# Expert weights loaded in halves: 1 MB transfers with a wait and a release for each half

## The reference, cut to what matters

```
for i in range(DEPTH):                      # 2 layers
    h = rmsnorm(x, norm_mix_g[i])
    x = x + (retention_mixer(h, ...) if i == 0 else conformer_conv_mixer(h, ...))
    h = rmsnorm(x, norm_ffn_g[i])
    x = x + hierarchical_moe(h, ...)        # 32 experts, each token goes to 2 of them
# for each expert e and each of its blocks of tokens:
    (silu(xblk @ w_gate[e]) * (xblk @ w_up[e])) @ w_down[e]   # 1024 -> 512 -> 1024
```

## Time and profile before

| | us |
|---|---|
| median of 3 runs (lowest, highest) | 1625.94 (1623.56, 1627.71) |
| the profiled execution's own time | 1625.24 |
| its span, first to last instruction | 1623.4 |
| TensorE busy | 1495.5 (92%) |
| VectorE busy | 989.1 (61%) |
| mean of the 16 DMA engines on the main queue | 67.4% of the span |

### The profile page before, as it was taken

One profiled execution on the slowest core, in us unless ns is written; L12 is line 12 of the kernel. 1 busy time (PEld: TensorE's weight loads), 2 busy tenths in 40 slices (PEclk: granted clock), 3 DMA queues, 4 the chain that ended last, 5 costly groups with the idle time before them and its releaser, 6 DMA issues.

```text
span 1623.4 us, 45311 instructions
## 1 busy us (share of the span) xinstructions
PE 1495.5 (92%) x18938; PEld 982.5 (61%) x18939; DVE 989.1 (61%) x1662; ACT 446.2 (27%) x731; POOL 423.7 (26%) x371
## 2 busy tenths in 40 slices
PE   7999999999989999998789899979999988889996
PEld 5868778688645555554445588747555555445553
DVE  4222022220378888776566889952788877668877
ACT  5242422322432222221112422154222212112222
POOL 3434334244101212121111255523021211112121
PEclk9999999999999999999999999999999999999998
DMA  9212212122299999999999620116399999999996
GB/s 377 85 64 71 93 53 104 52 104 104 87 377 428 429 428 428 429 428 428 429 429 426 277 100 20 41 57 266 118 417 430 428 429 429 428 428 430 428 428 271
DMA packets 33849, 457.60 MB, mean 282 GB/s; under 512 B 3840, under 2 KB 3968, under 8 KB 6400
## 3 DMA queue, kind: packets, MB, share of 16 engines
q1 hardware_dynamic: 33648, 456.57, 67.4%
q10 hardware_dynamic: 144, 0.18, 0.0%
HBM read 454.64 MB, written 2.10 MB: 281 GB/s over the span
## 4 chain that ended last, share of the span: by engine, by line
PE 66%; DMA 21%; DVE 10%; issue 1%; ACT 1%; SPq 0%; POOL 0%; DVEq 0%; ACTq 0%
PE ps L803 15%; PE ps L697 9%; PE ps L699 9%; PE ps L698 9%; DMA area_b<-w_gu 9%; PE ps L820 8%; PE ps L739 7%; PE ps L786 5%; DMA ring<-w_down 5%; DMA ring<-w_gu 4%; DVE area_c L1321 4%; DMA hT<-w_down 3%; PE ps L888 2%; DVE ring L1321 2%; PE ps L880 1%
## 5 line engine op out<-in xcount | busy, mean ns | idle before, releaser
L1159 DVE TENSOR_TENSOR x<-x,ps 128x1024 f32<-128x1024 f32 x384 | 450.9, 1216 | 90.7 <-PE ps L786 90.7
L456 POOL TENSOR_SCALAR slot_tok<-trig,slot_now 128x512 fp32r<-128x512 f32 x94 | 147.0, 1563 | 710.7 <-PE ps L786 710.7
L425 POOL TENSOR_TENSOR w_lo<-ring,w_hi 128x512 fp32r<-128x512 f32 x176 | 236.8, 1348 | 359.4 <-ACT w_hi L475 359.2
L803 PE MATMUL ps<-ring,hgT 128*32 128x256 f32 x4160 | 259.5, 391 | 48.4 <-DMA ring<-w_gu 28.6
L803 PEld LDWEIGHTS ps<-ring,hgT 128*32 128x32 f32 x4160 | 131.1, 111 | 145.0 <-issue 41.1
L475 ACT CAST w_hi<-ring 128x512 fp32r<-128x512 f32 x176 | 108.9, 623 | 346.8 <-PE ps L699 346.3
L739 PE MATMUL ps<-area_a,block_rows 128*32 128x256 f32 x3072 | 187.7, 386 | 0.6 <-DVE block_rows L1120 0.6
L549 ACT ACTIVATE y_hi<-ps,slots 128x256 fp32r<-128x256 f32 x94 | 44.5, 474 | 396.7 <-PE ps L820 396.7
L739 PEld LDWEIGHTS ps<-area_a,block_rows 128*32 128x32 f32 x3072 | 102.3, 113 | 72.1 <-issue 9.5
L820 PE MATMUL ps<-ring,aT_e 128*32 128x256 f32 x2080 | 125.7, 382 | 3.6 <-DMA ring<-w_down 3.6
L697 PE MATMUL ps<-w_hi,hT_hi 128*128 128x512 f32 x320 | 125.0, 391 | 2.9 <-DVE hT_lo L1351 2.9
(11 more groups left out here) (216 smaller groups left out, 1941.5 us busy)
## 6 DMA issues: line engine op xcount, KB each, us to landing
ring<-w_gu SPq DMA_DIRECT2D x88, 2048.0 KB, 28.1
ring<-w_down SPq DMA_DIRECT2D x44, 2048.0 KB, 29.0
area_c<-w_gu SPq DMA_DIRECT2D x20, 2048.0 KB, 29.3
area_b<-w_gu SPq DMA_DIRECT2D x20, 2048.0 KB, 31.8
hT<-w_down SPq DMA_DIRECT2D x20, 2048.0 KB, 32.4
ring<-w_pw SPq DMA_DIRECT2D x6, 2048.0 KB, 10.8
ring<-w_qk SPq DMA_DIRECT2D x4, 2048.0 KB, 8.4
ring<-w_v SPq DMA_DIRECT2D x4, 2048.0 KB, 8.7
```

What stands on the lines that cost most here:

```text
L425: nc.gpsimd.tensor_tensor(w_lo[:, place, :], ring[:, s, at:at + 512], w_hi[:, place, :].bitcast(F32), ALU.subtract).then_inc(lo_ready, 1)
L456: nc.gpsimd.tensor_scalar(slot_tok[:, :], tok_number, slot_now[:, 0:1], None, ALU.is_equal).then_inc(tok_hot[l], 1)
L803: last = nc.tensor.matmul(ps[32 * g:32 * g + 32, 2, 0:256], hgT[:, n * (KT // 2) + k, :], gate_up[n][:, k, :, g * P:(g + 1) * P], start=(n ...
L1159: return V.tensor_tensor(x[:, i, :].rearrange("p (g c) -> p g c", g=4), x[:, i, :].rearrange("p (g c) -> p g c", g=4), ps[:, bank:bank + 4 ...
```

## The change

Each expert load is cut in two of 1 MB: the first 2048 of the 4096 columns of a place ("front") and the last 2048 ("back"). The front ends on a new semaphore `front_loaded` of the place, the back on `slot_loaded`. TensorE waits for the front before the first half of its 16 matmuls on a place, and for the back before the second half. It counts up a new semaphore after each first half (`gu_first`, `gu_third`, `y_half`), and SyncE waits for that before the front of the later expert and for the old one before its back. The loads of retention and convolution weights are as before.

```
@@ sync queue @@
+            def load_front(s, w):
+                sp.dma_start(places[s][:, 0:SLOT // 2], w[:, 0:SLOT // 2]).then_inc(front_loaded[s], 16)
+            def load_back(s, w):
+                sp.dma_start(places[s][:, SLOT // 2:SLOT], w[:, SLOT // 2:SLOT]).then_inc(slot_loaded[s], 16)
+            def load_halves(s, w):
+                load_front(s, w)
+                load_back(s, w)
...
-                    load_slot(s, w[l, e])
+                    load_halves(s, w[l, e])
...
+                        sp.wait_ge(gu_first[l], upto)
+                        load_front(s_gu0, gu0_l[bass.ds(e * P, P), :])
                         sp.wait_ge(gu_half[l], upto)
-                        load_slot(s_gu0, gu0_l[bass.ds(e * P, P), :])
+                        load_back(s_gu0, gu0_l[bass.ds(e * P, P), :])
+                        sp.wait_ge(gu_third[l], upto)
+                        load_front(s_gu1, gu1_l[bass.ds(e * P, P), :])
                         sp.wait_ge(gu_mm[l], upto)
-                        load_slot(s_gu1, gu1_l[bass.ds(e * P, P), :])
+                        load_back(s_gu1, gu1_l[bass.ds(e * P, P), :])
+                        sp.wait_ge(y_half[l], upto)
+                        load_front(s_down, down_l[bass.ds(e * P, P), :])
                         sp.wait_ge(y_mm[l], upto)
-                        load_slot(s_down, down_l[bass.ds(e * P, P), :])
+                        load_back(s_down, down_l[bass.ds(e * P, P), :])
@@ tensor engine, one_block @@
-                    pe.wait_ge(slot_loaded[s], 16 * turn + (expert_base(l, s) + 16))
+                    pe.wait_ge(front_loaded[s], 16 * turn + (front_base(l, s) + 16))
                     for k in range(KT // 2):
+                        if k == KT // 4:
+                            last.then_inc((gu_first, gu_third)[n][l], 1)
+                            pe.wait_ge(slot_loaded[s], 16 * turn + (expert_base(l, s) + 16))
...
-                pe.wait_ge(slot_loaded[s_down], 16 * turn + (expert_base(l, s_down) + 16))
+                pe.wait_ge(front_loaded[s_down], 16 * turn + (front_base(l, s_down) + 16))
                 for k in range(4):
+                    if k == 2:
+                        last.then_inc(y_half[l], 1)
+                        pe.wait_ge(slot_loaded[s_down], 16 * turn + (expert_base(l, s_down) + 16))
```

More of the change, by code:

```diff
@@ L219, in program @@
         slot_loaded = sems("slot_loaded", 3 * DEPTH)
+        front_loaded = sems("front_loaded", 3 * DEPTH)
         x_loaded = sems("x_loaded", NT)
@@ L266, in program @@
             both(n) for n in ("slots_hot", "slots_spread", "tok_loaded", "slot_known", "tok_hot", "y_split", "y_rounded", "first_mm", "second_mm", "added"))
-        gu_half = both("gu_half")
+        gu_first, gu_half, gu_third, y_half = (both(n) for n in ("gu_first", "gu_half", "gu_third", "y_half"))
         hgT_ready, gu_mm, silu_ready, act_ready, aT_ready, y_mm = (
@@ L277, in expert_base, with front_base @@
             return after_ret[s] + l * (16 * experts + in_conv[s])
+        def front_base(l, s):
+            return l * 16 * len(range(s // 3, NE, DEPTH))
         slots_of = [(0, 1, 2), (3, 4, 5), (6, 7, 8)]
@@ L351, in _ @@
                 if l == 0:
-                    load_slot(6, w_gu0[l, 2])
-                    load_slot(7, w_gu1[l, 2])
+                    load_halves(6, w_gu0[l, 2])
+                    load_halves(7, w_gu1[l, 2])
                 sp.wait_ge(logitT_mm[l], 1)
-                load_slot(8, w_down[l, 2])
+                load_halves(8, w_down[l, 2])
                 sp.wait_ge(cum_ready[l], 1)
@@ L376, in _ @@
                     upto = sp.value_load(cum[0:1, e - 2:e - 1], min_val=1, max_val=NBLK - 1)
+                    sp.wait_ge(gu_first[l], upto)
+                    load_front(s_gu0, w_gu0[l, e])
                     sp.wait_ge(gu_half[l], upto)
-                    load_slot(s_gu0, w_gu0[l, e])
+                    load_back(s_gu0, w_gu0[l, e])
+                    sp.wait_ge(gu_third[l], upto)
+                    load_front(s_gu1, w_gu1[l, e])
                     sp.wait_ge(gu_mm[l], upto)
-                    load_slot(s_gu1, w_gu1[l, e])
+                    load_back(s_gu1, w_gu1[l, e])
+                    sp.wait_ge(y_half[l], upto)
+                    load_front(s_down, w_down[l, e])
                     sp.wait_ge(y_mm[l], upto)
-                    load_slot(s_down, w_down[l, e])
+                    load_back(s_down, w_down[l, e])
                 if l == 0:
@@ L400, in _ @@
                     sp.wait_ge(lo_ready, split)
-                    load_slot(3, w_gu0[1, 1])
+                    load_halves(3, w_gu0[1, 1])
                     sp.wait_ge(conv_mm, ROUNDS)
-                    load_slot(2, w_down[1, 0])
+                    load_halves(2, w_down[1, 0])
                     sp.wait_ge(hTlo_ready, 3 * KT)
-                    load_slot(6, w_gu0[1, 2])
-                    load_slot(7, w_gu1[1, 2])
+                    load_halves(6, w_gu0[1, 2])
+                    load_halves(7, w_gu1[1, 2])
                     sp.wait_ge(lo_ready, split + TILES)
-                    load_slot(0, w_gu0[1, 0])
+                    load_halves(0, w_gu0[1, 0])
                     sp.wait_ge(lo_ready, split + 2 * TILES)
-                    load_slot(1, w_gu1[1, 0])
+                    load_halves(1, w_gu1[1, 0])
                     sp.wait_ge(tile_used, NWT + split + 2 * TILES)
-                    load_slot(4, w_gu1[1, 1])
-                    load_slot(5, w_down[1, 1])
+                    load_halves(4, w_gu1[1, 1])
+                    load_halves(5, w_down[1, 1])
             for i in range(NT):
```

## The result

The changed kernel takes 1634.46 us in the median of 6 runs (1631.55 to 1636.94), the kernel before 1624.51 us (1623.56 to 1627.71, 6 runs). The ratio is 1.0055, interval 1.0044 to 1.0067: 8.9 us slower, between 7.1 and 10.9. (The forecast stood on a median of 1625.94 from three runs; against that the 1634.46 is 8.5 more.) The time lies inside the predicted range of 1622 to 1636, on the side that had 0.29; the forecast itself, +1.6 us, was not met. The rival "small pieces cost what the worst window shows" gave +7.8.

A forecast was written before the change was run, and what follows sets the result against it. The prediction took the weight stream, full from first refill to last landings, as the bound. Start -2.33, work left -2.47, stream length +5.95 and waits +0.5 gave +1.6 us: median 1627.6 us, range 1622 to 1636.

The forecast's parts named there:

- the side that had 0.29: Whole kernel: the outcome slower by over 0.3%, given a chance of 0.29.
- small pieces cost what the worst window shows: Expert streams in both layers: 0.071 us more a transfer, term 12.1, sum +7.8, time 1633.7 us; chance 0.22.
- What bounds the kernel: Expert stages: the weight stream at 428 GB/s, without pause from the first refill to the last landings.
- Start: First refill of each layer: issued 1.38 us earlier in layer 0, 0.95 in layer 1; gain 2.33 us.
- work left: Layer ends: half a product runs before the last back lands, saving 1.50 and 0.97 us; gain 2.47.
- The length of the stream: Expert streams: 8 KB pieces cost 0.035 us a transfer, over 170 transfers 5.95 us lost.
- The straight line: Piece cost, from x's 4 KB rows at 419 GB/s and 16 KB rows at 428: fixed part 4.4 ns.
- The added waits: TensorE: three more waits a block, 0.03 us each, 18 on the path: 0.5 us, at most 1.8.
- lower rate of alternating addresses: Expert streams: pieces 16 KB apart read slower; 1% of rate costs 8.3 us, time 1635.9; chance 0.08.
- free pieces: Expert streams: pieces cost nothing; 1622.8 us at 0.007 us a transfer, 1621.1 with free waits; chance 0.10.
- halves freed in mid-stage give no time: Mid-stage: TensorE's weight waits may fall, but the stream stays full, so no time and no case of its own.

The follow-up runs named there:

- experiment 1: Changed kernel with both halves issued where the whole was and TensorE waiting for both before its product: 1636.83 us, 1.0077 against the kernel before.
- Experiment 2: Kernel before with each expert place still one 2 MB transfer, but made of 8 KB pieces: 1637.35 us, ratio 1.0084.
- experiment 5: Kernel before with each expert place one 2 MB transfer made of 4 KB pieces: 1663.20 us, ratio 1.0241.
- experiment 3: Changed kernel with each half of a place stored as one contiguous 1 MB block in memory: 1632.54 us, 1.0053 against the kernel before.
- experiment 6: Kernel before with only TensorE's added waits and count-ups, 2 MB transfers kept: 1625.33 us, ratio 1.0002.
- experiment 4: As the size-only kernel, but places cut by partitions (0 to 63, 64 to 127), keeping 16 KB pieces: 2494.06 us, 1.5359 against the kernel before.
- experiment 10: Kernel before with the first six experts outside the loops of TensorE and SyncE, every load whole: 1627.93 us, ratio 1.0023.

## The prediction point by point: what held, and the step that failed

**What bounds the kernel** was right: the stream of weights, from the first refill to the last landings, without a gap. Experiments 1, 2 and 5 moved only its rate, by 1.4% (twice) and 4.2%, and the kernel followed with 12.5, 13.6 and 39 us. The size worked out from rate and count, 170 x 0.070 = 11.9 and 170 x 0.215 = 36.6, was right within 2.5 us.

**Start and work left** were about right: 1.70 and 0.85 us for 1.38 and 0.95 by the trace, and together with the work left 3.6 to 3.9 us by the time of experiment 1 against the changed kernel and against experiment 3 (each uncertain by about 3), where 4.8 less 0.5 for the waits were forecast. In layer 0 half a product does stand where a whole one stood. In layer 1 the last load bound within 0.3 us only, and in the changed kernel's trace it does not bind; in experiment 3's, with the same waits, it does, by 0.33 us, and half a product stands behind it.

**The length of the stream** is the step that failed, as "a 2 MB transfer ... 8 more cost 0.035 us (4.900 becomes 4.935, 425 GB/s)". It measured 0.070 and 422 GB/s. The straight line was sound, its 4 KB point was not: 419 GB/s from the loads of x. The experts' stream in 4 KB pieces gives 410 over 150 us (experiment 5), while the loads of x still read 419 in that very run. So one load's rate did not stand for another's with pieces of the same size. Neither the short window nor the share explains it. Windows of 2.5 us in the experts' stream read 405 to 413. And 419 divided by its share of 1.02 is 411, but the same division makes 398 of the stream's 410 with its 1.03. What differs is that x comes in transfers of 512 KB with one piece for each partition; whether that is the cause was not tried and stays open.

The price per piece is 8.8 to 9.0 ns, and my worst window gave 8.9. That is luck: it is half a microsecond at 410 GB/s out of the same loads of x, with 418 and 426 in the windows that follow. The range held because it reached up to this rival; the forecast in it did not. With that term the prediction's own sum is -2.33 - 2.47 + 11.9 + 0.5 = +7.6, inside the measured 7.1 to 10.9.

By the Trainium skill ("DMA: Bandwidth & Descriptors", "Measured (HBM→SBUF, 128 partitions, SWDGE, issued from GpSimd)") the floor of a small transfer comes to about 10.5 ns a packet, and by its section "Why small descriptors are slow" a packet has about 3 cycles of overhead, which the prediction put at an estimated 3.5 ns. The measured 9 ns lies nearer to the 10.5. So does the prediction's own 8.9, which it called nearer to the 3 cycles: that was a wrong reading.

**The added waits** cost nothing that can be measured (experiment 6); 0.5 us was allowed.

**The other rivals**: lower rate of alternating addresses fell (experiment 3), free pieces fell (422, not 428). That halves freed in mid-stage give no time was right: TensorE's waits for `ring` gate and up weights in layer 0 went from 10 of at most 2.3 us to 16 of at most 1.4, 17.9 us before and 18.3 after, and the stream was full all the same.

What stays open is 1 to 2 us: the kernels that measure price or gain alone are uncertain by 1.4 to 2.4 us each.

## What to carry to other kernels

Where the transfers are full from end to end, as here, only their start, their count of pieces and the work behind the last one count; earlier releases in mid-stage are worth nothing, and a finer cut pays its price on every transfer for a gain that falls due twice. Keep the contiguous run of each partition long (here 16 KB cost 4.900 us for 2 MB, 8 KB 4.970, 4 KB 5.115). Don't take the rate of one load for that of another because their pieces have the same size: a kernel with one long stream in the new size settles it.

## What the runs showed that I had not expected

**Half the partitions, half the rate.** A transfer to 64 partitions moved 216 GB/s with all engines full, for 428 to 128 partitions (experiment 4). Halves of partitions are no way to smaller transfers. Why was not tried.

**SyncE is held up when much is queued.** In the changed kernel an issue took up to 6.29 us in mid-stage, in the kernel before 0.33:

```profile
857.59 1.39 SPq L315 DMA_DIRECT2D ring<-w_gu  x1
859.02 0.44 SPq L319 DMA_DIRECT2D ring<-w_gu  x1
859.50 6.29 SPq L315 DMA_DIRECT2D ring<-w_gu  x1
865.84 2.13 SPq L319 DMA_DIRECT2D ring<-w_gu  x1
868.01 2.13 SPq L315 DMA_DIRECT2D ring<-w_down  x1
870.19 2.14 SPq L319 DMA_DIRECT2D ring<-w_down  x1
```

Landings come 26.68 us after the issue at 870.19, some eleven transfers of 1 MB at 2.485 us. The one at 844.00 in the earlier trace rows took 37.71 us, nearly eight of 2 MB. Experiment 2 tells transfers from pieces: it has as many transfers as the kernel before, each in 8 KB pieces, and there an issue took up to 10.88 us:

```profile
827.97 10.88 SPq L309 DMA_DIRECT2D ring<-w_down  x1
```

So what is limited is neither bytes nor transfers but something that grows with the count of pieces. In the chain such issues look like a cause; the DMA share of 1.01 shows that they cost nothing here.

**Code outside the loops was not free.** Six experts' instructions outside the loops, with sixteen more instruction packets, made the kernel 3.7 us slower (experiment 10). How they do it is not shown: the bytes of these packets cover an estimated 0.6 us.
